# A transformer block in split fp32 on one core: the norm weights come in the first transfer of x

## What is computed

```python
xn = rms_norm(h, norm_mix_g)                 # y * g, y = x * rsqrt(mean(x*x) + eps)
proj = xn @ w_in                             # q, k, v of two mixers and two gates
o_a = mixer_a(q_a, k_a, v_a, ...)            # windowed attention, sink, T5 bias
o_b = mixer_b(q_b, k_b, v_b, ...)            # chunked attention, relative bias
merged = sigmoid(g_a) * (o_a @ w_branch_a) + sigmoid(g_b) * (o_b @ w_branch_b)
h = h + merged @ w_out
hn = rms_norm(h, norm_ffn_g)
h = h + (silu(hn @ w_ffn_gate) * (hn @ w_ffn_up)) @ w_ffn_down
```

## Time and profile before

| | us |
|---|---|
| median of three runs | 1260.38 (1260.08 to 1260.4) |
| the profiled execution's own time | 1260.43 |
| its span (first to last instruction) | 1258.6 |
| PE busy | 1254.4 (100%) |
| DVE busy | 1051.8 (84%) |
| ACT busy | 757.7 (60%) |
| chain that ended last: PE | 99% |

### The profile page before, as it was taken

How to read it: one execution, slowest core, us unless ns; L and a number is a source line. 1 busy time by engine, 2 the same in 40 slices (tenths; PEclk the granted TensorE clock), 3 DMA queues, 4 the chain that set the end, 5 groups by cost and what they waited for, 6 DMA issues and landing times.

```text
span 1258.6 us, 14988 instructions
## 1 busy us (share of the span) xinstructions
PE 1254.4 (100%) x5870; PEld 1040.5 (83%) x5870; DVE 1051.8 (84%) x930; ACT 757.7 (60%) x765; POOL 93.3 (7%) x89
## 2 busy tenths in 40 slices
PE   9999999999999999999999999999999999999999
PEld 8888888888878888888888888888888888888887
DVE  6988887677889789779989888878898887888996
ACT  6766675566667555456656665556566555655653
POOL 3312312000000000000000000100000001000000
PEclk9999999999999999999999999999999999999999
DMA  9976683855357586956777768986686679866874
GB/s 353 318 249 192 203 264 118 269 164 160 113 187 244 173 299 211 339 165 191 247 251 232 253 183 251 281 248 220 203 263 242 197 217 304 260 219 191 278 217 118
DMA packets 137077, 285.98 MB, mean 227 GB/s; under 512 B 5408, under 2 KB 12080, under 8 KB 133424
## 3 DMA queue, kind: packets, MB, share of 16 engines
q1 hardware_dynamic: 129904, 252.20, 57.6%
q0 software_dynamic: 6784, 32.53, 13.8%
q10 hardware_dynamic: 320, 0.29, 0.1%
HBM read 251.42 MB, written 8.41 MB: 206 GB/s over the span
## 4 chain that ended last, share of the span: by engine, by line
PE 99%; DMA 0%; DVE 0%; ACT 0%; issue 0%; ACTq 0%; DVEq 0%
PE bank L2360 27%; PE bank L2365 27%; PE bank L2361 27%; PE bank L2303 5%; PE bank L2304 4%; PE bank L2311 4%; PE bank L2242 1%; PE bank L2255 1%; PE bank L2516 1%; PE bank L2271 1%; PE bank L2224 0%; DMA g_col<-in_gains 0%; PE bank L2529 0%; PE bank L2273 0%; PE bank L2214 0%; ACT xT_hi L1050 0%
## 5 line engine op out<-in xcount | busy, mean ns | idle before, releaser
L1805 DVE TENSOR_TENSOR u_lo<-quad,u_hi 128x2048 fp32r<-128x2048 f32 x245 | 556.9, 2289 | 109.4 <-ACT u_hi L1232 59.0
L1232 ACT ACTIVATE u_hi<-quad 128x2048 fp32r<-128x2048 f32 x250 | 475.5, 1915 | 282.7 <-PE bank L2365 161.0
L2360 PE MATMUL bank<-u_hi,xT_hi 128*128 128x512 f32 x676 | 263.3, 389 | 0.0
L2361 PE MATMUL bank<-u_hi,xT_lo 128*128 128x512 f32 x676 | 263.0, 389 | 0.0
L2365 PE MATMUL bank<-u_lo,xT_hi 128*128 128x512 f32 x740 | 198.1, 389 | 0.0
L2365 PEld LDWEIGHTS bank<-u_lo,xT_hi 128*128 128x128 f32 x740 | 138.8, 188 | 29.2 <-DVE u_lo L1805 0.5
L2360 PEld LDWEIGHTS bank<-u_hi,xT_hi 128*128 128x128 f32 x676 | 126.9, 188 | 26.2
L2361 PEld LDWEIGHTS bank<-u_hi,xT_lo 128*128 128x128 f32 x676 | 126.9, 188 | 26.2
L1543 DVE TENSOR_TENSOR w_lo<-raw,w_hi 128x1024 fp32r<-128x1024 f32 (+1 forms) x64 | 73.3, 1156 | 32.8 <-ACT w_hi L1035 31.9
L2361 PE MATMUL bank<-u_hi,fT_lo 128*128 128x512 f32 (+1 forms) x236 | 90.7, 385 | 0.0
L2360 PE MATMUL bank<-u_hi,fT_hi 128*128 128x512 f32 (+1 forms) x236 | 90.7, 385 | 0.0
(11 more groups left out here) (271 smaller groups left out, 1855.5 us busy)
## 6 DMA issues: line engine op xcount, KB each, us to landing
quad<-in_w_ffn_gate SPq DMA_DIRECT2D x44, 1024.0 KB, 6.8
quad<-in_w_ffn_up SPq DMA_DIRECT2D x44, 1024.0 KB, 6.1
quad<-in_w_ffn_down SPq DMA_DIRECT2D x44, 1024.0 KB, 6.0
quad<-in_w_in SPq DMA_DIRECT2D x41, 1024.0 KB, 6.9
quad<-quad POOLq DMA_DIRECT2D x24, 1024.0 KB, 8.2
raw<-in_w_in SPq DMA_DIRECT2D x16, 1024.0 KB, 5.7
quad<-in_w_out SPq DMA_DIRECT2D x16, 1024.0 KB, 5.2
raw<-in_w_branch_b SPq DMA_DIRECT2D x8, 1024.0 KB, 9.2
```

The source lines that it names most:

```text
L1232: A(st.hi[u.hi][:], st.quad[slot][:], ACT.Copy).then_inc(hi_ready, u.step)
L1805: V.tensor_tensor(st.lo[u.lo][:], st.quad[u.panel.slot[u.raw]][:], st.hi[u.hi][:].bitcast(F32), ALU.subtract).then_inc(lo_ready, u.step)
L2360: M(sums, a_hi(k), hi[:, w], start=start and k == 0, stop=False, skip_group_check=True)
L2361: M(sums, a_lo(k), hi[:, w], start=False, stop=False, skip_group_check=True)
```

## The change

The array `gains` and k-tile 0 of x become one array `head`: each partition has 56 values (the 52 of `gains` and 4 zeros of padding) and behind them the 256 values of x. It comes in one transfer of 312 values a partition as the first on SyncE's queue, and `g_col` and x's k-tile 0 are two views of where it lands. The transfer of `g_col` on ScalarE's queue, its semaphore and ScalarE's wait for it go; VectorE's wait is for `first_x_landed` instead. For the two views to be neighbours, `x_turned` moves to the lower half of its region (behind the gains) and `x_rows` to the upper one; `blocks` moves with `x_turned`. `SPINS` goes from 10 to 8.

```diff
-SPINS = 10
+SPINS = 8
...
+        ng = NG + HA + -(NG + HA) % 8
+        o_gains = take(ng * 4)
         o_att = take(2 * KT * S * 4)
+        assert o_att == o_gains + ng * 4
+        gains_x = at("gains_x", [P, ng + KT * S], F32, o_gains)
+        g_col = gains_x[:, 0:ng]
+        sink = g_col[:, NG:NG + HA]
...
-        x_rows = at("x_rows", [P, T, D], F32, o_att)
+        x_rows = at("x_rows", [P, T, D], F32, o_att + KT * S * 4)
...
-        blocks = at("blocks", [P, 4, COLS], F32, o_att + 2 * PAIRS * S * 4)
-        x_turned = at("x_turned", [P, KT, S], F32, o_att + KT * S * 4)
+        blocks = at("blocks", [P, 4, COLS], F32, o_att)
+        x_turned = gains_x[:, ng:].rearrange("p (k s) -> p k s", k=KT)
+        first_x = gains_x[:, 0:ng + S]
...
-        g_col = sb("g_col", [P, NG + HA])
-        sink = g_col[:, NG:NG + HA]
...
                 if k == 0:
-                    sp.dma_start(x_turned[:, 0, :], xT[0][:, 0]).then_inc(first_x_landed, 16)
+                    sp.dma_start(first_x, head).then_inc(first_x_landed, 16)
                     sp.dma_start(x_turned[:, 1, :], xT[0][:, 1]).then_inc(x_landed[0], 16)
...
             act.dma_start(raw[:, 0, 0:COLS], weights[first.weight][0, 0:P, bass.ds(first.col0, COLS)]).then_inc(half_w_landed[0], 16)
-            act.dma_start(g_col[:], gains).then_inc(g_landed, 16)
             act.dma_start(t5_sb[:], t5_heads).then_inc(t5_landed, 16)
             act.wait_ge(ident_ready, 1)
             A(sink_gap[:, 0, :], ident[:, 0:4], ACT.Copy)
-
-            act.wait_ge(g_landed, 16)
...
-            dve.wait_ge(g_landed, 16)
+            dve.wait_ge(first_x_landed, 16)
```

More of the change, by code:

```diff
@@ L377, in build @@
 def build(nc, x, w_in, rel_bias_b, w_branch_a, w_branch_b, w_out, w_ffn_gate, w_ffn_up, w_ffn_down,
-          xT, gains, t5_heads, out):
+          xT, head, t5_heads, out):
     _, S, D = x.shape
@@ L572, in build @@
         rows_landed = sem("rows_landed")
-        g_landed = sem("g_landed")
         t5_landed = sem("t5_landed")
@@ L2676, in by_k_tile, with gains_and_first @@
     return np.ascontiguousarray(x.T.reshape(d // (PIECE_KT * P), PIECE_KT, P, s).transpose(0, 2, 1, 3))
-def gain_columns(inputs):
+def gains_and_first(inputs, first):
     tiles = [inputs[name][0].reshape(-1, P).T for name in ("norm_mix_g", "norm_ffn_g")]
@@ L2683, in gain_columns @@
     sink = [np.broadcast_to(inputs["sink_a"][0], (P, inputs["sink_a"].shape[-1]))]
-    return np.ascontiguousarray(np.concatenate(tiles + pairs + sink, axis=1))
+    gains = np.concatenate(tiles + pairs + sink, axis=1)
+    gains = np.pad(gains, ((0, 0), (0, -gains.shape[1] % 8)))
+    return np.ascontiguousarray(np.concatenate([gains, first.reshape(P, -1)], axis=1))
 def t5_by_head(inputs):
@@ L2697 @@
     arrays, args = {}, []
-    laid_out = {"xT": by_k_tile(inputs["x"][0]), "gains": gain_columns(inputs), "t5_heads": t5_by_head(inputs)}
+    xT = by_k_tile(inputs["x"][0])
+    laid_out = {"xT": xT, "head": gains_and_first(inputs, xT[0][:, 0]), "t5_heads": t5_by_head(inputs)}
     for name in _INS + list(laid_out):
```

## The result

The changed kernel takes **1276.63 us** (median of 4 runs, 1276.31 to 1277.07) against 1260.3 us for the kernel before in the same comparison: a ratio of 1.013, 95% interval 1.0113 to 1.0148. The forecast was 1260.0 us and no difference. The profiled execution took 1277.07 us.

A forecast was written before the change was run, and what follows sets the result against it. TensorE bounds the kernel, busy 1254.4 of 1258.6 us in one unbroken row. Profiled 1260.43 us less 0.41 for the earlier start gives 1260.02 (1259.97 against the median), stated as 1260.0, "same"; range 1259.5 to 1260.7.

The forecast's parts named there:

- The head transfer: First transfer on its queue: 28 KB more cost 0.08 us, landing at 3.91; ScalarE starts 0.77 us earlier.
- Everything else is there by then: Before the first products: table load, copy and first weights are ready despite the earlier start; cost nothing.
- The margin called nil: Second half of first weights: there at 5.24, wanted near 5.27; a 0.2 us delay reaches TensorE only at 6.1 or later.
- Eight warming products: TensorE's start: eight end at 4.75, letting the row start at 5.19; ten would end at 5.68 and hold it back.
- The clock: TensorE's first products: clock rises at 7.19 regardless, so the 0.77 us won at low level leave a 0.41 us lead.
- rival A: TensorE's first products: clock rise moves with the work, 0.56 us of lead remain, 1259.9 us; chance 0.22.
- The moved tiles: `x_rows`, `x_turned`, `blocks`: no new wait; region start 224 B further on set at nothing, between 0.2 us gain or loss.
- Rival D: Memory: new places slow transfers or operands all through; 0.2% needs 2.5 us, about 2 ns per operation; chance 0.03.
- Rival B: Start: head lands near 4.4 to 4.7 or ScalarE waits for something else; 1260.2 to 1260.4 us; chance 0.13.
- Rival C: TensorE's start: longer idle time delays the clock's rise to 11.34, costing 2.1 us, 1262.1 us; chance 0.12.
- theory 1b: From the experiments, not the prediction: a product is slower if its stationary and moving operands' addresses, modulo 256, differ.

The follow-up runs named there:

- padded change: The change with the gains padded to 64 values (256 B a partition) instead of 56 (224 B), eight warming products kept: 1259.83 us, beside 1260.28 for the kernel before.
- hole of 32 B: Kernel before with only an unused 32 B a partition ahead of the region of `x_turned`, shifting all behind it: 1277.01 us.
- everything moved alike: Kernel before with all of its tiles 32 B further on: 1260.42 us beside 1260.28, ratio 1.0002.
- holes of 224, 64 and 128 B: Kernel before with only an unused hole of that size ahead of the region of `x_turned`: 1277.04, 1276.48 and 1276.33 us.
- stage: Kernel before with 32 B of hole ahead of the stage region and 224 B behind it, shifting only moving operands by 32 B: 1265.29 us.
- places: Kernel before with `x_turned` and `blocks` in the lower half of their region, `x_rows` in the upper, nothing shifted: 1260.25 us beside 1260.29.
- with five: The change with gains padded to 256 B and five warming products instead of eight: 1261.04 us.
- the hole before `xT`: Kernel before with a 32 B hole ahead of `xT_hi`, moving every stationary operand but `oT`, while weight slots 0 to 2 stay: 1287.71 us.

## Why the prediction was wrong

**The head transfer: right.** Landing 3.85 for 3.91, TensorE's first product at 5.22 for 5.19. The transfer took 3.12 us where the smaller one took 3.1, so neither its 28 KB more nor its odd rows can be told in it.

**Everything else is there by then: right in the changed kernel.** The margin called nil was nearly none. In the profiled execution of the padded change the second half of the first weights came later and the clock's rise earlier, and ScalarE began it at 5.85 and TensorE waited 0.21 us for it:

```profile
5.85 0.63 ACT L1061 ACTIVATE w_hi<-raw 128x512 fp32r<-128x512 f32 x1 [0.52 <-DMA raw<-in_w_in]
...
6.54 0.50 PE L2304 MATMUL bank<-w_hi,xT_hi 128*128 128x512 f32 x1 [0.21 <-ACT w_hi L1061]
```

**Eight warming products: wrong.** The prediction had this edit as what lets the first one count, and "without it the gain would be 5.96 - 5.68 = 0.28 us at most". In the padded change ten take 1259.86 us and eight 1259.83: no difference, and the first product starts 0.17 us later with ten (5.34 for 5.17), not 0.49. The step took the end of the last warming record for the earliest start of the next product; the first real product started at 5.34 although the record's modelled end is 5.69.

**The clock: right for the changed kernel, and by luck.** The rise came near 7.2, where the forecast had it, and the row was 0.36 us ahead at 8.07, forecast 0.41. But the term rests on one moment for the rise, read from one trace, and the moment differs between executions. The traces keep the granted clock as records with a start. The first record begins at 7.17 us in the kernel before (the prediction worked out 7.19) and at 7.23 in the change. In the kernels whose start is that of the kernel before, with ten warming products and a first product near 6.0, it begins at 7.05 (hole of 32 B), 6.83 (everything moved alike), 6.58, 6.29 and 5.00 (holes of 224, 64 and 128 B), 5.67 (stage) and 4.06 (places). The spacing goes with it; here is the hole of 224 B, to be read beside the earlier trace rows:

```profile
6.01 0.73 PE L2304 MATMUL bank<-w_hi,xT_hi 128*128 128x512 f32 x1 [0.33 <-DVE xT_lo L1553]
6.58 0.40 PE L2305 MATMUL bank<-w_hi,xT_lo 128*128 128x512 f32 x1
6.81 0.39 PE L2304 MATMUL bank<-w_hi,xT_hi 128*128 128x512 f32 x1
```

Of the kernels with ten warming products and an unchanged start, the kernel before has the latest rise of all. In the padded change's profile the second product follows 0.31 us behind the first at 5.17 and the third 0.23 behind that, so there the rise came before 5.5, earlier than even rival A has it. So 0.41 us is what the start gains where the rise falls at 7.2; one trace gave no ground to prefer it to rival A. Whether the moment of the rise is what spreads the runs of the padded change from 1259.35 to 1260.79 was not shown: its one profiled execution has an early rise and took 1260.07, more than the median. In the two kernels with a long idle time the profiled executions have both, the late rise and the longer time: the record begins at 10.58 with eight warming products alone (1262.10 us) and at 9.83 with five (1261.23 us), later than in every kernel above.

One reading of the earlier trace rows was also off. Both stretches end by 7.00, ahead of the rise, so they do not show the granted clock "on both sides of it". Behind it the stretch from 8 to 9 us reads 1.00 as well, but the stretches ahead of the first record read 1.00 only because there is no record there.

**The moved tiles: wrong, and this is the whole miss.** The step reads: "The region's start is 224 B further on; I set that at nothing, between a gain or loss of 0.2 us, as the row of TensorE would hide it." TensorE's row cannot hide what TensorE itself reads. The region and all behind it hold an operand of half of its products: 2,581 of the 5,118 distances belong to products with at least one moved operand, and by the table they cost 15 of the 17.2 us; the rest is in the products between them. Put at nothing, the term measures 16.8 us: 1277.04 with the hole of 224 B alone against 1260.29. The bound of 0.2 us was taken from no row. No row of the trace before could give one, since all operands stood alike to 256 B in it, and a term without any row should have had a wide range: 1 ns for each of 5,300 products is already 5 us.

**Rival D** had the place (memory, all through) and too small a chance: it looked for the cost in transfers and vector operations, which did not change (`u_lo` on VectorE is 2288 or 2289 ns in both), and spread 2.5 us over those. **Rival B** did not happen. **Rival C** did not happen in the change, whose idle time was 0.40 us, but does in the two runs with 1.15 and 1.54 us of it: then the row leaves the low level at 10.58 and 9.83 us by the clock records, where the rival had said 11.3.

## What to carry to other kernels

Where TensorE bounds a kernel, a change of memory layout is a change of its products. Before a tile is put between others, see what moves behind it, and keep the distances between stationary and moving operands at a multiple of 256 B; padding to that cost nothing here. Whoever finds a kernel slower with no wait in it counts the instructions in equal stretches and reads the distances between starts, sorted by operand, before looking at queues. Warming products are matched to the moment at which real work comes: taking two of ten away without bringing that moment forward cost 1.3 us here by the medians, in some of the runs and not in all.

## What the runs showed of the hardware

- A product of 512 columns (fp32r) starts 227 ns behind the last when its stationary and moving operand stand alike within 256 B, and 231 to 234 ns in the means of the groups, 5.6 to 6.4 ns more on average, when one of them is 32, 64, 128 or 224 B off the other (kernels with the four holes, with the hole before `xT`, and with the stage moved). A shift by 256 B costs nothing (the padding). Other distances, and the same with other types, were not tried.
- A common shift of all tiles by 32 B costs nothing (1.0002).
- A unit behind a mismatched one is slower too, though its own operands stand alike: `u_lo` on `xT` 228.4 ns in the changed kernel. Where both operands have moved alike amid mismatched ones, the mean is 229 to 231, though by theory 1b alone it would be 227 as with the common shift. Why, and what inside the chip sets the 256 B, no run here shows; the borders between units point to the next product's stationary operand in one trace and to the product's own in another.
- The moment at which TensorE's clock goes from the 1.2 to the 2.4 GHz level differs between executions with the same start: the first clock record begins anywhere from 4.06 to 7.17 us in eight traces with ten warming products and a first product near 6.0. A stretch of the profile ahead of that record reads 1.00 also where 512 columns take 0.43 us, the 1.2 GHz level; there only the spacing shows the level. The traces of the padded change and of the hole before `xT` have no record at all.
